# Mamba-2 mixer of a hybrid decoder layer: the 32 sample tokens held twice, on rows 0-31 and 32-63, their state update as two 32-row matmuls in two row groups, and the chunk outputs of two heads issued in turn

## The reference, cut to what matters

```python
def _ssd_chunked(x, dt, A, Bm, Cm, s0):
    Q = SSD_CHUNK if L % SSD_CHUNK == 0 else L        # prompt: 2 chunks of 128; sample: one of 4
    a_cs = jnp.cumsum(dt * A, axis=2)
    xdt = x * dt[..., None]
    seg = a_cs[:, :, :, None] - a_cs[:, :, None, :]
    decay = jnp.exp(jnp.where(causal, seg, -jnp.inf))
    cb = jnp.einsum('bclgn,bcsgn->bclsg', Cm, Bm)
    y_diag = jnp.einsum('bclsg,bclsgr,bcsgrp->bclgrp', cb, decay, xdt)
    decay_states = jnp.exp(a_cs[:, :, -1:] - a_cs)
    states = jnp.einsum('bcsgn,bcsgr,bcsgrp->bcgrpn', Bm, decay_states, xdt)
    ...                                               # s = chunk_decay * s + states, over the chunks
    y_off = jnp.einsum('bclgn,bcgrpn,bclgr->bclgrp', Cm, prev, jnp.exp(a_cs))
    return (y_diag + y_off).reshape(bt, L, G, R, P), final

# in _mamba2: xs, Bm, Cm are cuts of silu(causal_conv(xbc)); final is an output, (8, 16, 64, 128) for the sample
```

## Time and profile before

| | us |
|---|---|
| three timed runs | 1940.73, 1944.35, 1949.49 |
| median | 1944.35 |
| the profiled execution, its own time | 1939.3 |
| its span, first to last instruction | 1937.4 |
| PE busy in it | 1888.1 (97%) |
| DVE / ACT / POOL busy | 1088.7 / 703.6 / 235.1 |

### The profile page before, as it was taken

How to read it: one execution, slowest core, us unless ns; L and a number is a source line. 1 busy time by engine, 2 the same in 40 slices (tenths; PEclk the granted TensorE clock), 3 DMA queues, 4 the chain that set the end, 5 groups by cost and what they waited for, 6 DMA issues and landing times.

```text
span 1937.4 us, 32075 instructions
## 1 busy us (share of the span) xinstructions
PE 1888.1 (97%) x12311; PEld 1687.0 (87%) x12311; DVE 1088.7 (56%) x1923; ACT 703.6 (36%) x1051; POOL 235.1 (12%) x257
## 2 busy tenths in 40 slices
PE   7999999999999999999899999999999999999998
PEld 4866677777777899996599999999999999999997
DVE  4796697764444646444335655555555555555544
ACT  2100142533333434334223443344444444444444
POOL 1013300002022233000013100000000000002200
PEclk9999999999899999999999999999999999999999
DMA  6332353455445656647745555555555555554553
GB/s 205 98 98 88 98 195 114 128 159 174 141 153 184 211 171 233 206 141 292 295 133 166 152 168 163 162 163 163 163 166 164 165 148 160 166 164 152 162 163 104
DMA packets 157954, 316.45 MB, mean 163 GB/s; under 512 B 16938, under 2 KB 39482, under 8 KB 152931
## 3 DMA queue, kind: packets, MB, share of 16 engines
q1 hardware_dynamic: 136146, 296.01, 48.8%
q10 hardware_dynamic: 21723, 19.27, 3.1%
HBM read 300.78 MB, written 14.89 MB: 163 GB/s over the span
## 4 chain that ended last, share of the span: by engine, by line
PE 87%; DVE 3%; ACT 2%; DMA 1%; issue 0%; ACTq 0%; SPq 0%; DVEq 0%
PE bank L706 23%; PE bank L1127 19%; PE bank L1129 19%; PE bank L1128 19%; PE bank L1228 2%; PE bank L1240 1%; PE bank L775 1%; DMA out_s_ssd<-s 1%; PE bank L760 1%; PE bank L1250 1%; DVE raw_lo L2305 1%; DVE wlo L2462 0%; DMA kv<-in_cache_mem_v 0%; PE bank L1070 0%; DVE hlo L2484 0%
## 5 line engine op out<-in xcount | busy, mean ns | idle before, releaser
L1127 PE MATMUL bank<-hhi,whi 128*128 128x288 f32 x2128 | 632.5, 297 | 7.6 <-DVE wlo L2462 6.1
L1128 PE MATMUL bank<-hlo,whi 128*128 128x288 f32 x2128 | 629.1, 296 | 0.0
L1129 PE MATMUL bank<-hhi,wlo 128*128 128x288 f32 x2128 | 627.0, 295 | 0.0
L2462 DVE TENSOR_TENSOR wlo<-raw,whi 128x1024 fp32r<-128x1024 f32 (+1 forms) x270 | 330.1, 1224 | 382.4 <-ACT whi L1617 382.1
L1617 ACT ACTIVATE whi<-raw 128x1024 fp32r<-128x1024 f32 (+1 forms) x270 | 283.1, 1049 | 511.9 <-PE bank L1129 510.0
L1127 PEld LDWEIGHTS bank<-hhi,whi 128*128 128x128 f32 x2128 | 400.1, 188 | 9.0 <-DVE wlo L2462 7.0
L1129 PEld LDWEIGHTS bank<-hhi,wlo 128*128 128x128 f32 x2128 | 402.2, 189 | 0.0
L1128 PEld LDWEIGHTS bank<-hlo,whi 128*128 128x128 f32 x2128 | 400.9, 188 | 0.1
L706 PE MATMUL bank<-hT,raw 128*128 128x288 f32 x1024 | 263.8, 416 | 1.2 <-DVE hT L1955 1.2
L706 PEld LDWEIGHTS bank<-hT,raw 128*128 128x128 f32 x1024 | 196.0, 194 | 60.3 <-issue 7.1
L1127 PE MATMUL bank<-ahi,whi 128*128 128x288 f32 x688 | 203.9, 296 | 3.5 <-DVE alo L2702 1.6
(11 more groups left out here) (474 smaller groups left out, 1978.8 us busy)
## 6 DMA issues: line engine op xcount, KB each, us to landing
raw<-in_ffn_w_down SPq DMA_DIRECT2D x86, 512.0 KB, 3.7
raw<-in_ffn_w_gate SPq DMA_DIRECT2D x80, 512.0 KB, 3.6
raw<-in_ffn_w_up SPq DMA_DIRECT2D x80, 512.0 KB, 3.6
raw<-in_w_in SPq DMA_DIRECT2D x64, 512.0 KB, 3.6
raw<-in_xa_wk SPq DMA_DIRECT2D x32, 512.0 KB, 3.8
raw<-in_xa_wv SPq DMA_DIRECT2D x32, 512.0 KB, 4.3
raw<-in_w_out SPq DMA_DIRECT2D x32, 512.0 KB, 3.8
raw<-in_xa_wq SPq DMA_DIRECT2D x32, 512.0 KB, 3.8
```

The source lines that it names most:

```text
L1127: pe.matmul(out, lhsT=wh[:, wo:wo + P], rhs=xh, start=first, stop=False)
L1128: pe.matmul(out, lhsT=wh[:, wo:wo + P], rhs=xl, start=False, stop=False)
L1129: return pe.matmul(out, lhsT=wl[:, wo:wo + P], rhs=xh, start=False, stop=last)
L2462: tt(wlo[:, s % 2, wsl], raw[:, s % 4, wsl], whi[:, s % 2, wsl].bitcast(F32), ALU.subtract)\
```

## The change

- The turned sample tokens are written twice, on output rows 0-31 and 32-63. The transposes of the sample part become plain matmuls with the identity as moving data (`twice`), one at column 0 and one at column 32 of the array. `tokT`, `xdt`, `btok` and `xds` then hold the sample on 64 rows; the DVE instructions on them work on 64 rows instead of 32.
- `bm` is 64 rows x 4 sequences instead of 32 rows x 8: rows 0-31 hold sequences 0-3, rows 32-63 sequences 4-7. Its table `bsel` is copied from `bmask` by POOL at the start, two small copies.
- The update's second matmul takes `xds` and `bm` from rows 32-63 and sits at row 32 of the array. The first stays at row 0. The banks are the same.
- The chunk outputs alternate between the heads (c outside, h inside). There is one wait for `mixed` in front of all instead of one ahead of each head. Each head's last matmul still raises `y_mm`.

```diff
@@ POOL, at the start, in the loop over h that builds bmask
+                if h < 2:
+                    pool.tensor_copy(bsel[NS * h:NS * (h + 1), :], rows_h[:, 4 * h:4 * h + 4]).then_inc(S("bsel"), 1)
+                    pool.wait_ge(*at("bsel", h + 1))
@@ PE
+            def twice(out, cols, unit):
+                for r in (0, NS):
+                    q = pe.matmul(out[r:r + NS, :], lhsT=cols, rhs=unit, start=True, stop=True, tile_position=(0, r))
+                return q
@@ PE, token_columns
-                    for c in range(3):
-                        w = P if c < 2 else NS
-                        q = pe.transpose(B[4][0:w, (q3 * 3 + c) * NH:(q3 * 3 + c + 1) * NH],
-                                         dtr[:, q3, c * P:c * P + w], ident[0:NH, 0:NH])
+                    for c in range(2):
+                        pe.transpose(B[4][:, (q3 * 3 + c) * NH:(q3 * 3 + c + 1) * NH],
+                                     dtr[:, q3, c * P:(c + 1) * P], ident[0:NH, 0:NH])
+                    twice(B[4][:, (q3 * 3 + 2) * NH:(q3 * 3 + 3) * NH], dtr[:, q3, NP:T], ident[0:NH, 0:NH])
@@ PE, token_rows, for x and for B
+            def turn_tokens(out, tile, c):
+                if c < 2:
+                    return pe.transpose(out, tile[:, c * P:(c + 1) * P], ident[:, :])
+                return twice(out, tile[:, NP:T], ident[:, :])
@@ PE, ssd_b
-                for h in range(2):
-                    hd = 2 * j + h
-                    r = HP * h
-                    pe.wait_ge(*at("mixed", 4 * j + 2 * h + 2))
-                    for c in range(2):
-                        ...
-                    q = pe.matmul(B[5][r:r + HP, NP:T], ...)
-                    q.then_inc(S("y_mm"), 1)
+                pe.wait_ge(*at("mixed", 4 * j + 4))
+                for c in range(3):
+                    for h in range(2):
+                        hd = 2 * j + h
+                        r = HP * h
+                        if c < 2:
+                            ...
+                        else:
+                            pe.matmul(B[5][r:r + HP, NP:T], ...).then_inc(S("y_mm"), 1)
@@ PE, ssd_b, the update
-                for i in range(2):
-                    q = mm(B[6 + i][:, :], xds[0:NS, j * P:(j + 1) * P],
-                           bm[:, 4 * i:4 * i + 4, :].rearrange("p b n -> p (b n)"))
+                for r in range(2):
+                    rows = slice(NS * r, NS * (r + 1))
+                    q = pe.matmul(B[6 + r][:, :],
+                                  lhsT=xds[rows, j * P:(j + 1) * P],
+                                  rhs=bm[rows, :, :].rearrange("p b n -> p (b n)"),
+                                  start=True, stop=True, tile_position=(NS * r, 0))
@@ DVE, masked_b
-                tt(bm[:, :, :], btok[0:NS, 2, g, :].unsqueeze(1).to_broadcast([NS, NB, NST]),
-                   bmask[0:NS, :].unsqueeze(2).to_broadcast([NS, NB, NST]), ALU.mult).then_inc(S("masked_b"), 1)
+                tt(bm[:, :, :], btok[0:2 * NS, 2, g, :].unsqueeze(1).to_broadcast([2 * NS, 4, NST]),
+                   bsel[:, :].unsqueeze(2).to_broadcast([2 * NS, 4, NST]), ALU.mult).then_inc(S("masked_b"), 1)
```

More of the change, by code:

```diff
@@ L119, in hymba_step @@
         bmask = sb("bmask", [P, NB])
+        bsel = sb("bsel", [2 * NS, 4])
         g4 = sb("g4", [P, 4])
@@ L248, in hymba_step @@
         s0T = alloc(lev, "s0T", [P, NB, P])
-        bm = alloc(lev, "bm", [NS, NB, NST])
+        bm = alloc(lev, "bm", [2 * NS, 4, NST])
         lev.close()
@@ L960, in token_rows @@
                 for g in range(2):
[L961 removed]
+                    q = turn_tokens(bk[:, g * P:(g + 1) * P], xc[:, 8 + g, :], c)
                 q.then_inc(S("b_t"), 1)
@@ L1064, in ssd_b @@
                     pe.wait_ge(*at("btok", 3))
-                for h in range(2):
-                    hd = 2 * j + h
-                    r = HP * h
-                    pe.wait_ge(*at("mixed", 4 * j + 2 * h + 2))
-                    for c in range(2):
[L1070 to L1073, removed]
-                    q.then_inc(S("y_mm"), 1)
+                pe.wait_ge(*at("mixed", 4 * j + 4))
[4 more added lines that the diff above has]
+                        if c < 2:
+                            pe.matmul(B[5][r:r + HP, c * P:(c + 1) * P], lhsT=xdt[:, c, hd * HP:(hd + 1) * HP],
+                                      rhs=dec[:, h, c * P:(c + 1) * P], start=True, stop=True, tile_position=(0, r))
+                        else:
+                            pe.matmul(B[5][r:r + HP, NP:T], lhsT=xdt[0:NS, 2, hd * HP:(hd + 1) * HP],
+                                      rhs=decs[:, h, :], start=True, stop=True, tile_position=(0, r))\
+                                .then_inc(S("y_mm"), 1)
                 pe.wait_ge(*at("eb_ready", j + 1))
@@ L2331, in token_rows @@
             def token_rows(c):
-                w = P if c < 2 else NS
+                w = P if c < 2 else 2 * NS
                 for hf in range(2):
@@ L2375, in sample_tokens @@
                 v.wait_ge(*at("btok", 3))
+                v.wait_ge(*at("bsel", 2))
                 masked_b(0)
-                tt(v3(xds[0:NS, :], HP), v3(xdt[0:NS, 2, :], HP), per_head(2, 2, NS), ALU.mult).then_inc(S("xds"), 1)
+                tt(v3(xds[0:2 * NS, :], HP), v3(xdt[0:2 * NS, 2, :], HP), per_head(2, 2, 2 * NS), ALU.mult)                    .then_inc(S("xds"), 1)
             def ssd_a(j):
```

5 lines of the change are left out of this document (2 added, 3 removed).

## The result

| | before | after |
|---|---|---|
| timed runs, median | 1942.92 (1940.73 to 1949.49, 4 runs) | 1918.15 (1911.69 to 1923.43, 4 runs) |
| ratio, 95% interval | | 0.9865 [0.9844, 0.9886] |
| profiled execution / its span | 1939.3 / 1937.4 | 1911.7 / 1909.6 |

The change makes the kernel 22 to 30 us faster; 17 were predicted. The predicted time, 1927, is 9 us above the median and its range holds it. The profiled execution of the changed kernel is the fastest of its four timed runs, so what its profile shows is the change at its best.

What follows compares the result with a forecast made beforehand. PE, busy for 97% of the span, was taken as the bound. PE work of -11.0 us and a clock gain of -6.0 summed to -17.0, so 1927 us beside the median 1944.35, range 1914 to 1941.

Steps and rivals of the forecast that it cites:

- Chunk outputs, -6.5: In `ssd_b`, both heads' column groups run at once: 0.81 us saved per round, 6.5 us in eight rounds.
- Update, -6.4: State update's two matmuls at rows 0 and 32 run side by side: 0.8 us saved per round, 6.4 in all.
- Tokens, +1.9: Writing sample tokens twice costs PE 1.1 us in `token_rows(2)` and 0.8 us in `token_columns`.
- Sum of the work, -11.0: PE work in the K/V stage: -6.5 chunk outputs, -6.4 update, +1.1 and +0.8 tokens, together -11.0 us.
- The clock, -6: Eight half-clock stretches around the rounds' updates lose 15.3 us; a shorter thin stretch wins back 6 us.
- Rival 1: The clock falls as often as before, so only PE work is saved: 1933 us; chance 0.25.
- Rival 2: Update's row groups do not run side by side at 512 columns, clock stays: -4.6 us, 1940; chance 0.10.
- Rival 3: Engines preparing slabs or emptying PSUM become the bound and take back the matmuls' gain: 1942 us; chance 0.10.
- Rival 4: PE's clock stays low a second time after every round: 11.7 us slower, 1956 us; chance 0.05.

Runs made afterwards that it cites:

- chunk_only: Kernel before with only the chunk outputs of the two heads in turn; median 1934.84 us, ratio to before 0.9944.
- update_only: Changed kernel with the chunk outputs back in their old order, doubled tokens and two-row-group update kept; median 1927.43 us, ratio to before 0.9899.
- double_only: Changed kernel with old chunk order and old update, leaving only the doubled sample tokens; median 1940.62 us, ratio to before 0.999.
- four: Changed kernel carried to four row groups: tokens on 128 rows, update as four matmuls of 256 columns; median 1920.09 us, ratio to before 0.9893.
- after: The changed kernel itself, against the kernel before; median 1918.15 us over 4 runs, ratio 0.9865.
- again: The changed kernel, unaltered, in a further set of 6 runs; median 1917.5 us, ratio to before 0.9885.
- late: Kernel before with only the update moved behind the next slab, no instruction removed; median 1928.01 us, ratio to before 0.9912.
- after_three: Changed kernel with chunk outputs one slab earlier and update one slab later, so three pieces per round; median 1914.88 us, ratio to before 0.9853.
- early: Kernel before with only the chunk outputs issued one slab earlier, no matmul saved; median 1932.27 us, ratio to before 0.9944.
- pad_dense: Changed kernel plus one full-array fp32 matmul of 512 columns ahead of each round's update; median 1930.85 us, ratio to before 0.9943.
- pad_fast: Changed kernel plus four full-array split-operand matmuls of the K/V kind ahead of each round's update; median 1931.28 us, ratio to before 0.9941.
- after_late: Changed kernel with the update moved one slab later; median 1913.6 us, ratio to before 0.9855.

## Why the prediction was right, and where it was off

- **Chunk outputs, -6.5: right.** 1.62 to 0.82 us per round is 6.4 in eight rounds; by `chunk_only` the work is 5.0 less in the profile and 5.8 over all timed runs. The attention's four column groups foretold two. The single wait for `mixed` cost nothing.
- **Update, -6.4: right.** 1.91 to 1.05 us is 6.9 in eight rounds; by the difference between `update_only` and `double_only` 6.2. The first and the last of the four records start 0.5 us apart (431.4 and 431.9), where one behind the other makes it 1.4. The Trainium skill ("TensorE: Matmul & The Clock Gate", Part 3) gave 7.6 in place of 6.4; the timeline stands between, with 0.1 us left per round. In the trace of the kernel before, the steady distance of two such records is 0.43, and the first and the last take 0.53 and 0.52 up to what follows: 0.1 for each change of shape, paid once for a group of records however many lie side by side. With four groups the same rule would have, as an estimate, 0.48 us for a matmul of 256 columns in each, a quarter of the 1.91 that two matmuls of 512 take in one group; `four` took 0.65, so what the rule leaves out grows in share as the matmuls get short.
- **Tokens, +1.9: right in the timelines.** +0.7 in `token_columns` (0.8 predicted), +1.3 in `token_rows(2)` (1.1 predicted). `double_only` shows no second wait behind them; over all timed runs its time at full clock is 0.3 us above that of the kernel before, less than the 2.0 of the timelines.
- **Sum of the work, -11.0: right.** The four timelines sum to -11.3, and over all timed runs the time at full clock fell by 11.5 (1902.5 to 1891.0, `after` and `again` together). The stage less h/2 of the two profiles says -9.6; PE's pauses in it are 7.3 and 6.9 us (1.5 less waiting for slabs, the new 1.19 for POOL's square), which doesn't account for the difference, and for it I have no place. The prediction adds the two rows of waits, 9.3 + 6.5; they are largely the same pauses seen twice, and nothing in its sum hangs on that.
- **The clock, -6: this is the step that was off.** The prediction took less than half of at most 15.3 us. The half-clock time fell from 37.4 to 6.8 us, and half of the difference is 15.3: by coincidence exactly the ceiling, though two other stretches remained and two of those not counted went. Over all timed runs, `after` and `again` together, the loss fell from 38.6 to 24.5, by 14.1 where 6 were forecast: that is the mis-sized term. The two that were not counted had been ascribed to pauses of PE. In `after` PE pauses for 2.02 us at 500.6, and no low stretch follows:

```profile
502.63 0.50 PE L710 MATMUL bank<-khi,mhi 128*128 128x512 f32 x1 [2.02 <-DVE raw_lo L2325]
```

```profile
504.00:507.40 3.40, 3.40 (x29) 1.00 0.57 191
```

  So a pause of that length isn't enough by itself; `late`, `update_only` and others have the same one without a fall. It can go with one all the same: besides the kernel before, the clock falls within 1 us of the end of PE's pauses of 2.87 and 2.04 us in `four` and of 2.22 in `after_three`. That the clock follows the small work was in the prediction, and `late` shows it. The reason that the prediction gave, the thin stretch of `s0T` matmuls and update, is not shown: `early` leaves it whole and still loses 7.7 us less, and a full pad does the harm of a thin one. So the sign of the term was forecast by a reason that holds at best in part, and its size was guessed between two ends; the guess was too low. This term makes nearly the whole difference between -17 and the measured -22 to -30.
- **Rival 1** (clock as before, 1933): refuted by the loss over all timed runs, 24.5 against 38.6; two stretches were left in the profile. **Rival 2** (row groups one behind the other, 1940): refuted by the timeline. **Rival 3** (the splitting engines become the bound, 1942): refuted, PE's own waits for slabs fell from 6.5 to 5.0 us; and DVE and ACT empty the banks beside PE as before. `four` may show how it begins: 8.5 us of such waits. **Rival 4** (a second low stretch after each round, 1956): refuted; it would have had the sign of the clock term wrong.
- **What sets the clock stays open.** Shown: it depends on how the small work stands between the slabs (`late` and `early`, with no matmul saved) and on adding 0.8 to 1.1 us of any kind to it (three pads, 5 to 7 us more loss). Not enough by themselves: how thin the work is (`pad_dense`), how slow (`pad_fast`), how long it is in one piece (`early` beside `after`). A rule made of two of these would fit what was measured, but no run here tests one.

**The best version.** `after_late` and `after_three` have the lowest medians, 1913.6 and 1914.9, against 1918.15 and 1917.5 for the changed kernel. Their intervals, 0.9855 [0.9833, 0.9876] and 0.9853 [0.9832, 0.9875], overlap with the changed kernel's, 0.9865 [0.9844, 0.9886]. Both beat the kernel before; a lead over the changed one is not shown in the times, though the loss to the clock is 6 to 7 us less in both.

## What to carry to other kernels

Small matmuls that need only some rows or columns of the array are worth issuing in turn over two groups, as long as the operands can be had on the second group's rows for less than is saved: here 2.0 us of doubling bought 6.9. Then read the granted clock behind every such place: in this kernel the change gave back at least as much clock (14.1 us) as it saved work (11.5), and moving the update by one slab, with nothing removed, made 0.9%. Don't judge the clock by one profile: two runs of the same kernel can differ by 10 us of it, and the span and mean clock of every timed run tell what is usual. Price such a clock term by an experiment that only moves work, and not by a share of the ceiling.

## What the runs showed of the hardware

- Two row groups with 512 columns of fp32 and 32 rows of weights run at once: four instructions in 1.05 us, the two of a pair 0.007 us apart, 1.91 in one group. Four row groups with 256 columns: eight instructions in 0.65 us.
- Forty fp32 instructions of 128 columns, in two column groups pair by pair (the two of one matmul, then those of the other group), take 2.31 us, 0.058 each; in one place such an instruction takes 0.10.
- A full-array fp32 matmul of 512 columns (two instructions) ahead of the packed update takes 1.0 us, about as long as four of the K/V kind (1.1).
- The granted clock falls to its lower level (1.2 GHz) for 3.4 or 6.8 us at a time with PE busy all through, as at 460.40 in `early`, and a pause of 2.0 us need not bring this about. From one run to the next of the same kernel the loss to the clock varies: the spans of 63 runs differ by up to 19.5 us, their span times clock by 6.0.
